# The double norm's squares summed by POOL in place of TensorE, and the state groups' inputs moved behind a projection

## The reference, cut to what matters

```
x = x + m_x[:, 5] * _conv_ffn(h2, ...)      # "down": D_FF -> 1024, in two halves
x = _rmsnorm(x, g_final)                    # end of the first block
h = rms_norm(x, mix_norm_g)                 # start of the second
proj = h @ w_in                             # u, q, k, v, f, two gates
y_ssm = s5_branch(u, ...)                   # 2048 complex states in 16 groups of 128
q = head_rms_norm(q, q_g)                   # each head by its own root mean square
```

## Time and profile before

| | |
|---|---|
| time, median of 3 runs | 3240.05 us (3239.52 to 3242.59) |
| the profiled execution: its time | 3241.85 us |
| its span in the trace | 3240.0 us |
| granted TensorE clock, mean | 0.993 |
| TensorE busy | 3171.5 us, 98% |
| DVE busy | 2060.2 us, 64% |
| POOL busy | 425.9 us, 13% |

### The profile page before, as it was taken

How to read it: one execution, slowest core, us unless ns; L and a number is a source line. 1 busy time by engine, 2 the same in 40 slices (tenths; PEclk the granted TensorE clock), 3 DMA queues, 4 the chain that set the end, 5 groups by cost and what they waited for, 6 DMA issues and landing times.

```text
span 3240.0 us, 37547 instructions
## 1 busy us (share of the span) xinstructions
PE 3171.5 (98%) x14084; PEld 2513.9 (78%) x14084; DVE 2060.2 (64%) x3455; ACT 1248.9 (39%) x2295; POOL 425.9 (13%) x186
## 2 busy tenths in 40 slices
PE   8999999999999999999999999999999999999999
PEld 7877778878778656767778888888888888888887
DVE  7678354367898899546646896777761455555554
ACT  4365222233223322235433335999982211111111
POOL 0000000014132000000002444333334000000000
PEclk9999999999999999999999999999999999999999
DMA  5243324332242454221122444676867555555553
GB/s 211 59 126 124 102 71 146 121 109 95 72 155 84 143 172 134 72 79 52 59 91 95 133 139 137 176 206 193 219 177 231 205 187 190 188 189 190 187 190 115
DMA packets 285845, 455.77 MB, mean 141 GB/s; under 512 B 148952, under 2 KB 156248, under 8 KB 285280
## 3 DMA queue, kind: packets, MB, share of 16 engines
q1 hardware_dynamic: 150560, 409.84, 37.9%
q10 hardware_dynamic: 135104, 43.52, 6.0%
HBM read 372.01 MB, written 81.26 MB: 140 GB/s over the span
## 4 chain that ended last, share of the span: by engine, by line
PE 91%; DVE 6%; ACT 1%; issue 1%; DMA 0%; POOL 0%; ACTq 0%; DVEq 0%
PE psum L644 91%; DVE wl L1489 1%; ACT wh L1077 1%; DVE yb L1701 0%; DVE psum L1865 0%; DVE trig L1584 0%; DVE lb L1692 0%; DVE st L1942 0%; DVE cs L1699 0%; DVE y L1703 0%; DVE trig L1587 0%; DVE trig L1586 0%; DVE trig L1589 0%; DVE trigw L1588 0%; DVE trigw L1585 0%
## 5 line engine op out<-in xcount | busy, mean ns | idle before, releaser
L644 PE MATMUL psum<-h_hi,wh 128*128 128x512 f32 x2144 | 857.0, 400 | 32.7 <-DVE h_lo L1633 13.2
L1489 DVE TENSOR_TENSOR wl<-ring,wh 128x1024 fp32r<-128x1024 f32 (+2 forms) x322 | 375.7, 1171 | 747.4 <-ACT wh L1077 746.4
L644 PE MATMUL psum<-h_lo,wh 128*128 128x512 f32 x2144 | 849.2, 396 | 0.0
L644 PE MATMUL psum<-h_hi,wl 128*128 128x512 f32 x2144 | 849.2, 396 | 0.0
L1077 ACT ACTIVATE wh<-ring 128x1024 fp32r<-128x1024 f32 (+2 forms) x492 | 504.6, 1027 | 813.5 <-PE psum L644 789.3
L2235 POOL TENSOR_TENSOR wl<-ring,wh 128x1024 fp32r<-128x1024 f32 x170 | 423.0, 2489 | 1784.3 <-ACT wh L1077 1784.3
L644 PEld LDWEIGHTS psum<-h_hi,wh 128*128 128x128 f32 x2144 | 406.4, 190 | 133.1 <-issue 40.6
L644 PEld LDWEIGHTS psum<-h_hi,wl 128*128 128x128 f32 x2144 | 405.8, 189 | 95.8
L644 PEld LDWEIGHTS psum<-h_lo,wh 128*128 128x128 f32 x2144 | 406.3, 190 | 88.5 <-issue 1.7
L644 PE MATMUL psum<-ews_hi,wh 128*128 128x512 f32 x1024 | 404.1, 395 | 0.7 <-ACT ga L1456 0.7
L644 PE MATMUL psum<-ews_hi,wl 128*128 128x512 f32 x1024 | 404.0, 395 | 0.0
(11 more groups left out here) (384 smaller groups left out, 3776.6 us busy)
## 6 DMA issues: line engine op xcount, KB each, us to landing
ring<-tables SPq DMA_DIRECT2D x256, 512.0 KB, 3.6
acts_scratch<-ga SPq DMA_DIRECT2D x128, 256.0 KB, 2.2
gates_scratch<-stage ACTq DMA_DIRECT2D x8, 4096.0 KB, 26.2
abuf<-acts_scratch SPq DMA_DIRECT2D x128, 256.0 KB, 3.8
gbuf<-gates_scratch SPq DMA_DIRECT2D x128, 256.0 KB, 4.0
ring<-w_up SPq DMA_DIRECT2D x44, 512.0 KB, 3.6
ring<-w_modb SPq DMA_DIRECT2D x32, 512.0 KB, 3.6
ring<-w_moda SPq DMA_DIRECT2D x16, 512.0 KB, 5.6
```

The lines of the kernel that those rows point to most:

```text
L644: return nc.tensor.matmul(out, lhsT, rhs, start=first, stop=last, **kw)
L1489: TT(wl, slot(t, 0, size[t]), wh.bitcast(F32), ALU.subtract).then_inc(S("low_by_ve"), 1)
```

## The change

Two things are changed.

One: of the sixteen squares of the double norm, POOL adds those of chunks 1 to 6 to those of chunk 0 (twelve additions of 128x512 fp32, two inputs and the output in SBUF, into `nrm[2][3]` and `nrm[2][4]`), behind its last low part of the feed-forward stage. TensorE then sums four tiles and not sixteen: the two that POOL made, and the squares of chunk 7. `folded_sums` now serves one bank or two, and `column_sums` goes. The squares of a chunk wait for POOL's addition and not for TensorE's sum.

Two: in the state stage the first projection comes ahead of `states_in(0)`, and so on: for each c the order is `states_out(c-2)`, `q_sum(c-1)`, `BESIDE[c]`, `q_row(c-10)`, `states_in(c)`. The last `states_out` stands behind the projection `gs2`. DVE's low part in group c is of the tile three behind `BESIDE[c]` and not `BESIDE[c-1]`. DVE's other work keeps its places.

```diff
-            def column_sums(k, first, banks, roots, c):
-
-                if c == 0:
-                    pe.wait_ge(S("sd_done"), roots)
+            def folded_sums(k, first, banks, roots, rest):
+
+                n = len(banks)
                 for j, bk in enumerate(banks):
-                    n = first + c * len(banks) + j
-                    pe.wait_ge(S("sq_ready"), n + 1)
-                    mm(psum[:, bk, :], ones[:, :], nrm[k][n % 2], c == 0, c == KD - 1).then_inc(S("sq_used"), 1)
-
-            def folded_sums(k, first, bk, roots, rest):
-
-                if rest:
-                    pe.wait_ge(S("sq_ready"), first + KD)
-                    mm(psum[:, bk, :], ones[:, :], nrm[k][1], False, True).then_inc(S("sq_used"), 1)
-                else:
-                    pe.wait_ge(S("sd_done"), roots)
-                    pe.wait_ge(S("sq_used"), first + KD - 2)
-                    mm(psum[:, bk, :], ones[:, :], nrm[k][3], True, False).then_inc(S("sq_used"), 1)
+                    if rest:
+                        pe.wait_ge(S("sq_ready"), first + n * (KD - 1) + j + 1)
+                        mm(psum[:, bk, :], ones[:, :], nrm[k][j if n == 2 else 1], False, True)\
+                            .then_inc(S("sq_used"), 1)
+                    else:
+                        pe.wait_ge(S("sd_done"), roots)
+                        pe.wait_ge(S("sq_used"), first + n * (KD - 2))
+                        mm(psum[:, bk, :], ones[:, :], nrm[k][3 + j], True, False).then_inc(S("sq_used"), 1)
...
-                    if len(banks) == 2 and n >= 2:
-                        column_sums(k, first, banks, roots, n - 2)
-                    if len(banks) == 1 and n >= KD:
-                        folded_sums(k, first, banks[0], roots, n == KD + 1)
+                    if n >= KD:
+                        folded_sums(k, first, banks, roots, n == KD + 1)
...
-            states_in(0)
             for c in range(NS):
-                if c:
-                    states_out(c - 1)
+                if c >= 2:
+                    states_out(c - 2)
                 if 1 <= c <= HEADS:
                     q_sum(c - 1)
                 project(BESIDE[c], h)
                 if c >= QROWS:
                     q_row(c - QROWS)
-                if c + 1 < NS:
-                    states_in(c + 1)
-            states_out(NS - 1)
+                states_in(c)
+            states_out(NS - 2)
             for n in range(NS - QROWS, HEADS):
                 q_row(n)
 
             for name in AFTER:
                 if name[:3] != "glu":
                     project(name, h)
+                    if name == AFTER[0]:
+                        states_out(NS - 1)
                     continue
...
                         for j in range(2):
-                            k = 2 * KD + 2 * n + j
-                            wait(act, S("sq_used"), k - 1)
-                            A(nrm[2][k % 2], x[:, n, :], ACT.Square, scale=gfe[:, n:n + 1] if j else 1.0)\
+                            act.wait_ge(S("sq_used"), 2 * KD + max(2 * (n - 2) + j + 1, 0))
+                            A(nrm[2][j if n else 3 + j], x[:, n, :], ACT.Square, scale=gfe[:, n:n + 1] if j else 1.0)\
                                 .then_inc(S("sq_ready"), 1)
...
-                if c:
-                    low_after(TILE[BESIDE[c - 1]])
+                low_after(TILE[BESIDE[c]])
...
             for name in FFN_BY_GP:
                 low(name)
+
+            for c in range(1, KD - 1):
+                for j in range(2):
+                    gp.wait_ge(S("sq_ready"), 2 * KD + 2 * c + j + 1)
+                    wait(gp, S("sq_used"), 2 * KD + 2 * (c - 1) + j if c > 1 else 0)
+                    g.tensor_tensor(nrm[2][3 + j], nrm[2][3 + j], nrm[2][j], ALU.add).then_inc(S("sq_used"), 1)
```

## The result

The kernel after takes 3270.56 us (median of 4 runs, 3269.16 to 3272.09), the kernel before 3241.32 us in the same session (4 runs, 3239.52 to 3244.77): ratio 1.0092, 95% interval 1.0077 to 1.0107, 29 us slower. The forecast was 3264 us with a range from 3247 to 3275. The profiled execution took 3271.69 us (span 3269.9, 29.9 more than before).

The account below looks back on a forecast made before the run. TensorE, busy 98% of the span, was taken to bound the kernel, with DVE's lateness deciding its waits. Double norm +6 and state stage +18 made 24 us, hence 3264 us; range 3254 to 3274, from 3247 with (a).

Parts of the forecast that it names:

- The double norm, +6 us: End of feed-forward stage: POOL's additions hold DVE, whose late weight parts delay TensorE; +5.6 us, +6 with clock, bounds -4 and +10.
- The state stage, +18 us: State groups in the new order: waits 19.7, less 3.1, plus 5 for clock, less 3.6 at the start; bounds +13 and +23.
- The start: Group 0 of the state stage: 5.35 us of stall and clock go, about 1.7 us of waiting stays; -3.6 us.
- Rows 2 to 5: `q_row(2)` to `q_row(5)` wait for the bank `q_norm` frees: four rounds 1.2 us longer, 1.9 with `skip`; 5.7 us.
- `q_row(0)`: First head row comes before DVE's reciprocal of the heads' root, ready at 14.0 against TensorE's 9.5; 4.4 us wait.
- `q_row(7)`: Last head row waits for `q_norm(4)` behind group 15, whose inputs went out late; 6.2 us.
- `gs3`: End of state stage: needs the bank of `q_norm(5)`, behind `skip(3)` and `halve(3)` waiting for `states_out(15)`; 3.4 us.
- Lower clock: State stage: one row's worth of slower matmuls after each of three gaps over 3 us, 3 x 1.65; +5 us.
- (a): Rival: POOL does not hold DVE, as its additions start while DVE waits; -4.3 + 18, 3253.7 us; chance 0.12.
- (b): Rival: the heads' rows in the state stage do not wait, DVE being through; +6 - 3.6, 3242.5 us; chance 0.06.
- (c): Rival: only TensorE's queue counts, so all the sums' time and the starting stall come off; 3225 us; chance 0.08.
- (d): Rival: more than counted, lower clock after every gap and full holds; over 3275 us; chance 0.08.

Follow-up runs that it names:

- experiment 3: Kernel of experiment 1 with each POOL addition replaced by two fills that read nothing; 3242.6 us (one run).
- Experiment 5: Kernel of experiment 2 with DVE's `q_norm` of each head one group earlier; 3243.33 us, ratio 1.0004 to the kernel before.
- experiment 1: POOL's additions as in the change, state groups as in the kernel before; 3247.5 us, ratio 1.0019.
- experiment 4: Kernel of experiment 1 with the twelve additions made by DVE instead of POOL; 3246.41 us, ratio 1.0014 to the kernel before.
- experiment 2: The order alone: kernel before with the change's new state-stage order, all sixteen sums on TensorE; 3265.66 us, ratio 1.0073.
- experiment 6: Kernel of experiment 5 with DVE's reciprocal of the heads' root moved ahead of group 9's sums and scan; 3238.22 us, ratio 0.9986 to the kernel before.
- experiment 8: Kernel of experiment 6 with the double norm's squares in four buffers instead of two; 3234.5 us, ratio 0.9982 to the kernel before.
- experiment 9: Kernel of experiment 8 with each `q_sum` behind its group's projection instead of ahead; 3237.2 us, ratio 0.9986 to the kernel before.

## Why the prediction was right

**The double norm, +6 us: measured +6.0.** DVE's side holds step by step. An addition of POOL takes 1.27 to 1.29 us in eight cases and 1.56 to 1.74 in four (taken: 1.2), DVE loses 0.98 to 1.11 for each (taken: 1.0), ten of them fall on its table instructions and cost it 10.2 us (taken: 10). The weight parts of `down1_7` come at 1107.46, less the 0.7 by which the stretch began later 1106.8 (taken: 1106.6). The root is at 1117.39, without the 0.7 at 1116.7 (taken: 1116.4 and a little clock). TensorE's side differs inside the stretch: its waits are four of 2.3 to 3.3 us and not five with a last one of 5, and it ran at a lower clock in between. The same 232 records are busy for 59.8 us here (granted clock 0.95) and 56.7 in experiment 3 (1.00). That did not move the end, which DVE's chain sets. Experiment 3 shows the lower bound as well: without the hold the stretch gains 5.6 us, where the prediction's bound was 4.3; the quicker fills may explain the 1.3 us between them.

**The state stage, +18 us: measured +21.** By terms:

- The start, -3.6. The waits of 0.61 and 3.24 us and the lower clock behind the second, 5.35 us in all, are gone, and one of 1.7 us is new: -3.65. The size was right and the place was not. I had the rest of the wait at the first turned tile; it is `q_sum(0)`, which used to stand behind group 0's stall and now comes before ACT has squared head 0.
- Rows 2 to 5, 5.7 taken (its own terms, three of 1.2 and one of 1.9, make 5.5): 1.19, 0.65, 1.20 and 1.24, together 4.3. The extra 0.7 for the round with `skip` did not come; a round with 0.65 came in its place.
- `q_row(0)`, 4.4 taken: 4.63.
- `q_row(7)`, 6.2 taken (10.9 less 4.1 would be 6.8; how the rows' being late came in was not written down): 4.13. DVE was ready when it should be, 11.0 us behind the inputs of group 15 (1324.56 to 1335.59). What was mis-sized is TensorE's own work in that time, 6.9 us and not 4.1: `states_out(14)` held it for 5.16 us at the lower clock in place of 3.0, and the row of `q_row(6)` took 1.12 in place of 0.5. So the slower clock took 2.1 us of this wait for itself.
- `gs3`, 3.4 taken: 3.47.
- Lower clock, 5 taken. The waits make 16.5 us, less 3.1 for the old wait and its clock and less 3.65 for the start: 9.7. The stage lost 21.0, so some 11 us are matmuls that ran slower. Experiment 5 shows 8.8 of them behind the six `q_norm` waits alone. I had charged one slow row after each gap over 3 us and nothing after the short ones. But 1.19 us was followed by eight matmuls of 4.84 and 1.24 us by 5.23. The row of before that I used for the price, 1.29 us of waiting and 5.40, had been such a short gap itself; the reading of it was at fault, not the row.

So the mechanism held and two terms were mis-sized in opposite directions, `q_row(7)` and the rows by -3.5 and the clock by +6. That is the difference between +18 and +21, and that the sum came out as near as this is in part luck.

**What the forecast did not have** is the rest of the 29.9 us, 0.7 ahead of the stretches and 2.3 behind them. Of the 2.3, 1.1 lie between the first scores and the next norm: 122.2 us after, 121.1 before. Another 1.0 lie in the 106 us behind that (1593.7 to 1700.0 before, 1622.5 to 1729.8 after). TensorE's waits have the same places and the same lengths to 0.1 us in both; its matmuls take longer, 1.0 us in each of the two, and in the first the granted clock shows it (0.97 after, 0.99 before). The first of these stretches takes from 120.9 to 123.9 us over the kernels of this study, with and without POOL's additions, though the three longest are kernels with changed sums (experiments 1, 3 and 4). Whether something ties it to them or whether it is chance stays open; no run was made for it.

**The rivals.** (a) fell with the 1.67 us rows. (b) fell with the waits of L1919. (c), TensorE's queue as all that counts, fell doubly: TensorE has 24 matmuls less and ends 30 us later. Yet experiment 3 shows its condition in part: where DVE is not held, 5.6 us come off, of the 10.3 that twelve sums take at 0.86 each, as TensorE then waits 5.0 us for DVE. (d) was not reached, but the clock, its mechanism, was what I had too small.

## What to carry to other kernels

Before work is handed to an idle engine, price what it does to the engines that work beside it, at the place where it runs: here POOL's addition cost DVE 0.98 to 1.11 us, more than DVE's own 0.69 us for the same addition, and DVE was what TensorE's next weights waited for. When a producer's place in an in-order queue is moved, list everything between the old place and the new one that waits for the consumer's side: the move of the inputs was worth 3.4 us, and the head rows that it passed cost 24 until two DVE steps were moved too. And in a kernel whose TensorE is busy 98% of the time, a wait has a second price, the slower matmuls behind it: here 8.8 us for 11.5 us of waiting in the order alone. It can't be told for a single short wait: of three of 1.2 us, two had it and one did not.

## What the runs showed of the hardware that I had not expected

- Short gaps and the clock: after one of 0.65 us the next eight matmuls ran at the full clock (3.60 us); after 0.95 (experiment 6), 1.19 and 1.24 us they took 5.30, 4.84 and 5.23 us; but after the wait of 1.20 us at 1311.46 they took 3.60. The sharpest case is one and the same wait for `turned`, 0.95 us long, in experiment 8 and in experiment 9:

```profile
1248.93 3.70 PE L644 MATMUL psum<-turned,outw 128*128 128x512 f32 x8 [0.95 <-DVE turned L1961]
```

```profile
1248.51 5.40 PE L644 MATMUL psum<-turned,outw 128*128 128x512 f32 x8 [0.95 <-DVE turned L1961]
```

  So the length of the gap alone doesn't decide it; what does was not found. All in all, 11.5 us of waiting took 8.8 us of clock with it (experiments 2 and 5).
- A POOL addition did not only hold large DVE instructions. Timeline of DVE after, with instructions of 128x4, 128x128 and 128x256 that stood beside one:

```profile
1066.28 1.27 DVE L1578 TENSOR_TENSOR trig<-trig,small 128x4 f32<-128x4 f32 x1
...
1077.31 0.29 DVE L1577 TENSOR_TENSOR trig<-trig,trigw 128x128 f32<-128x128 f32 x1
1077.63 1.29 DVE L1578 TENSOR_TENSOR trig<-trig,small 128x128 f32<-128x128 f32 x1
1078.96 1.40 DVE L1579 TENSOR_TENSOR trigw<-trig,small 128x128 f32<-128x128 f32 x1
...
1097.98 1.48 DVE L1577 TENSOR_TENSOR trig<-trig,trigw 128x256 f32<-128x256 f32 x1
1099.49 1.40 DVE L1578 TENSOR_TENSOR trig<-trig,small 128x256 f32<-128x256 f32 x1
```

  Without a neighbour they take 0.17, 0.29 and 0.42 us (the one of 128x4 also in experiment 3). So the loss is 1.0 to 1.1 us whatever the size of DVE's own instruction, for all ten that were held.
- POOL seems to be held in its turn. The four additions that met DVE's instructions of 128x512 took 1.56 to 1.74 us, the other eight 1.27 to 1.29.
